# Second attention: bias, scale and row maximum with the sink in one VectorE instruction per head, and pairs of heads begun one or two chunks apart

## The chip, the core and the metric

The kernel runs on one core of one Trainium2 chip. The metric is the device time of one execution in microseconds (us). Five engines run their own instruction streams and meet through semaphores: TensorE (PE in the profile; its weight loads are PEld), VectorE (DVE), ScalarE (ACT), GpSimd (POOL) and SyncE (SP), which issues the loads of the weights.

## The reference

Two transformer blocks of width 2048 run one after the other on 256 positions, all in float32. The first has two attention branches, gates and a gated network. The second begins with a sliding-window attention of 32 query heads and 8 key heads of 64 values, and that is the part that the change touches:

```python
s = jnp.einsum('bnqhgd,bnshd->bnhgqs', q, kb).astype(jnp.float32) * HEAD_DIM ** -0.5 + bias
s = jnp.where(mask[None, :, None, None], s, -jnp.inf)
```

The bias comes from a table by distance. Each head also has a sink logit, which takes part in the softmax (in its maximum and in its sum) and in nothing else. The scale is 1/8. After it come the output product, a norm, a convolution network and its down product.

## The kernel before, in words

**The stream of weights.** All products with weights are one list of 812 chunks. A chunk is two tiles of 128 x 512 of some weight (1024 floats per partition). SyncE loads it to `raw`; ACT casts it to a rounded copy `whi` (L796); DVE subtracts that from the original to get the rest, `wlo` (L1147); PE multiplies with three matmuls of 512 columns per tile and half of the positions (L1755 to L1757), 12 for a chunk. `whi` and `wlo` have three places each, and so the cast of chunk t+2 waits until PE is through with chunk t-1.

**Side steps.** Everything else is cut into named steps, which `side_steps` puts at chunk numbers. Each engine goes through the chunks in order. At chunk t, ACT and DVE first do the cast and the subtraction of chunk t+2, ACT then empties finished product banks where there are any, and then each does its part of the steps at t, in the order in which they were put. PE does the matmuls of chunk t and then its part of the steps at t. No engine steps over an instruction that waits.

**The second attention.** It works on 16 pairs of heads, in four groups c of four pairs e (pair i = 4c + e). A pair goes through ten steps at ten chunks in a row:

- `pscore`: PE makes the scores in two banks, two heads of 128 x 128 in one and of 128 x 256 in the other (eight matmuls).
- `psoft`: DVE adds scale and bias and takes the maximum (L1494 to L1516). This is the step that is changed.
- `pexp`: ACT makes the exponentials with their sums (L1033) and that of the sink (L1036).
- `pprob`, `pscale`: DVE scales a third of them by 1 over the sum (L1520, L1522, L1158), ACT the rest (L764).
- `pptr`: PE turns six tiles of 128 x 128 in two banks (L1817).
- `ppcp`: ACT copies them out (`PH`), and DVE takes the rest (`PL`, L1529).
- `ppv`: PE multiplies with the values (L1986, L1987).
- `py`, `pz`: ACT and DVE add the two halves (`YS`, L1536) and split the sum (`YH`, `YL`, L1539).

Before each group come `qtr` (PE turns the queries, source `NAT`) and, a chunk later, `qcp` (`QP`, ACT and DVE, four instructions each for the two).

**Four side banks.** Side steps share PSUM banks 4 to 7. `side_banks` hands them out in turn, in the order of the steps, so a new order of the steps also changes who follows whom on a bank. PE waits in front of a use until the reader of the bank's last use is through: `psoft` frees a `pscore` (semaphore `s_pbias`), `ppcp` a `pptr` (`s_pptV`), `py` a `ppv` (`s_ys`), `qcp` a `qtr` (`s_q`).

**Biases.** GpSimd loads the bias tiles of a group to `BT`, which has two places. The loads for groups 2 and 3 wait for `psoft` of the last pair of groups 0 and 1.

Of the kernel before, what the change touches and what calls it, by code (L numbers as in the profile page):

```python
# [12 lines left out]
ALU = mybir.AluOpType  # L13
ACT = mybir.ActivationFunctionType
AX = mybir.AxisListType.X

P = 128
D = 2048
S = 256
# [176 lines left out]
def side_steps(chunks):  # L196
# [3 lines left out]
    def put(t, *step):  # L200
        at[t].append(step)
# [26 lines left out]
    for n in range(16):  # L228
        t0 = (64 if n < 8 else 108) + 3 * (n % 8)
# [60 lines left out]
    for j in range(4):  # L290
        put(478 + j, "ktr", j)
        put(479 + j, "kcp", j)
    for c, (t0, t1) in enumerate(((484, 487), (500, 503), (508, 512), (516, 521))):
        for b in range(2):
            put(t0 + 1, "qtr", 2 * c + b)
        for b in range(2):
            put(t0 + 2, "qcp", 2 * c + b)
        stages = ("pscore", "psoft", "pexp", "pprob", "pscale", "pptr", "ppcp", "ppv", "py", "pz")
        for e in range(4):
            for j, name in enumerate(stages):  # L300
                put(t1 + e + j, name, 4 * c + e)
    put(544, "gain", 2)
    for name, i in (("busy", 0), ("rs", 6), ("update", 0), ("Ttr", 16), ("Ttr", 17), ("Tsp", 16), ("Tsp", 17),
                    ("update", 1), ("sq6", 0)):
# [59 lines left out]
def build(nc, A):  # L364
    ctx = ExitStack()
    with ctx:
# [10 lines left out]
        def sems(names):  # L377
            return [ctx.enter_context(nc.semaphore("s_" + n)) for n in names.split()]
# [73 lines left out]
        SK = sb("SK", [P, 32])  # L452
# [47 lines left out]
        s_sig, s_mix, s_xb = sems("sig mix xb")  # L500

        s_dupA, s_ktr, s_khi, s_k, s_qtr, s_qhi, s_q = sems("dupA ktr khi k qtr qhi q")
        s_psc, s_pbias, s_pmax, s_psink, s_pneg, s_pexp, s_psum, s_prcp, s_ppv = sems(
            "psc pbias pmax psink pneg pexp psum prcp ppv")
        s_pprobV, s_pprobA, s_pptr, s_pptA, s_pptV, s_yt, s_ys, s_yhi2, s_Y2 = sems(
            "pprobV pprobA pptr pptA pptV yt ys yhi2 Y2")
        s_mg, s_upd, s_busy, s_rowd, s_rowm, s_R = sems("mg upd busy rowd rowm R")
# [84 lines left out]
        def side_freed(use):  # L592

            name, i, b = use
            if name == "bias":
                return s_biasln, 1
            if name == "ctr":
                return s_C, 2 * i + 2
            if name == "krtr":
                return s_kr, 2  # L600
            if name == "qktr":
                return s_qk, i + 1
            if name == "score":
                return s_msk, i + 1
            if name == "ptr":
                return s_pt, i + 1
            if name == "pv":
                return s_y, i + 1
            if name == "uqtr":
                return s_uq, i + 1  # L610
            if name == "mktr":
                return s_mk, i + 1
            if name == "mtr":
                return s_M, 2 * i + 2
            if name == "Ttr":
                return s_T, 16 + 2 * i + 2
            if name == "htr":
                return s_H, i + 1
            if name == "ktr":
                return s_k, i + 1  # L620
            if name == "qtr":
                return s_q, 2 * i + 2
            if name == "pscore":
                return s_pbias, 2 * i + 1 + b
            if name == "pptr":
                return s_pptV, 2 * i + 1 + b
            if name == "ppv":
                return s_ys, 2 * i + 2
            if name == "busy":
                return s_busy, i + 1  # L630
            return s_R, 1

        def bt_view(c, e, n):
            base = BT[:, c % 2, 2 * e:2 * e + 2, 0:n]
            pat = [list(z) for z in base.ap]
            pat[-1] = [-1, n]
            return bass.AP(base.tensor, base.offset + n - 1, pat)
# [56 lines left out]
        def gpsimd_program(eng):  # L694
            po = Seat(eng)
# [44 lines left out]
            load_bias(0)  # L740
            load_bias(1)
            row_rstd(5)
            po.wait_ge(s_pbias, 8)
            load_bias(2)
            po.wait_ge(s_pbias, 16)
            load_bias(3)
            po.wait_ge(s_qtr, 8)
            eng.dma_start(GB[:, :], bass.AP(A["norm_g_2"].tensor, D, [[0, P], [1, D]])).then_inc(l_g1, 16)
# [11 lines left out]
        def scalar_program(eng):  # L760
            ac = Seat(eng)
# [128 lines left out]
            def side(name, i, t):  # L890
# [138 lines left out]
                elif name == "pexp":  # L1029
                    s, a = pair_scores(i), AS[:, i % 6, :]  # L1030
                    ac.wait_ge(s_pneg, i + 1)
                    for z, (lo, hi) in enumerate(PAIR_PARTS):
                        eng.activation(s[:, lo:hi], s[:, lo:hi], ACT.Exp, bias=a[:, 12 + z:13 + z], scale=1.0,  # L1033
                                       accum_out=a[:, 8 + z:9 + z]).then_inc(s_pexp, 1)
                    ac.wait_ge(s_psink, 2 * i + 2)
                    eng.activation(a[:, 4:8], a[:, 4:8], ACT.Exp, bias=0.0, scale=1.0).then_inc(s_pexp, 1)  # L1036
                elif name == "pscale":
                    s, a = pair_scores(i), AS[:, i % 6, :]
# [52 lines left out]
            c = 2  # L1091
# [17 lines left out]
        def vector_program(eng):  # L1109
# [209 lines left out]
            def side(name, i, t):  # L1319
# [164 lines left out]
                elif name == "psoft":  # L1484
# [5 lines left out]
                        ve.wait_ge(s_pptr, 2 * (i - 4) + 2)  # L1490
                    else:
                        ve.wait_ge(s_mm, upto[IN2])
                    ve.wait_ge(s_psc, 2 * i + 1)
                    eng.scalar_tensor_tensor(out=s[:, 0:S].rearrange("p (h n) -> p h n", h=2),  # L1494
                                             in0=b0[:, 0:S].rearrange("p (h n) -> p h n", h=2), scalar=0.125,
                                             in1=bt_view(c, e, P), op0=ALU.mult, op1=ALU.add).then_inc(s_pbias, 1)
                    ve.wait_ge(s_psc, 2 * i + 2)
                    eng.scalar_tensor_tensor(out=s[:, S:768].rearrange("p (h n) -> p h n", h=2),
                                             in0=b1.rearrange("p (h n) -> p h n", h=2), scalar=0.125,
                                             in1=bt_view(c, e, S), op0=ALU.mult, op1=ALU.add).then_inc(s_pbias, 1)  # L1500
                    if i >= 6:
                        ve.wait_ge(s_pprobA, 2 * (i - 6) + 2)
                        ve.wait_ge(s_pprobV, 2 * (i - 6) + 2)
                    ve.wait_ge(s_pbias, 2 * i + 1)
                    eng.reduce_max(a[:, 0:2], s[:, 0:S].rearrange("p (h n) -> p h n", h=2), AX).then_inc(s_pmax, 1)
                    ve.wait_ge(s_pbias, 2 * i + 2)
                    eng.reduce_max(a[:, 2:4], s[:, S:768].rearrange("p (h n) -> p h n", h=2), AX).then_inc(s_pmax, 1)
                    av = a[:, 0:4].rearrange("p (t h) -> p t h", t=2)
                    dv = a[:, 4:8].rearrange("p (t h) -> p t h", t=2)
                    sk = SK[:, 2 * i:2 * i + 2].unsqueeze(1).to_broadcast([P, 2, 2])  # L1510
                    ve.wait_ge(s_pmax, 2 * i + 2)
                    ve.wait_ge(l_sk, 16)
                    eng.tensor_tensor(av, av, sk, ALU.max).then_inc(s_psink, 1)
                    ve.wait_ge(s_psink, 2 * i + 1)
                    eng.tensor_tensor(dv, sk, av, ALU.subtract).then_inc(s_psink, 1)
                    eng.tensor_scalar(a[:, 12:16], a[:, 0:4], -1.0, None, ALU.mult).then_inc(s_pneg, 1)  # L1516
                elif name == "pprob":
# [547 lines left out]
def constants():  # L2065

    f = np.float32
    c = np.zeros((P, 560), f)
    c[:, 0:128] = np.eye(P, dtype=f)
    tri = np.where(np.arange(P)[None, :] <= np.arange(P)[:, None], 0.0, NEG).astype(f)  # L2070
    c[:, 128:256] = tri
    c[:, 384:512] = tri
    for o, d in ((512, 32), (528, 64)):
        fr = f(500000.0) ** (-np.arange(0, d, 2, dtype=f) / f(d))
        c[:, o:o + d // 2] = fr.astype(f)[None, :]
    b = np.zeros((32, 768), f)
    b[:, 384:768] = NEG
    for i in range(127, 255):
        n = i - 127
        if n < 16:  # L2080
            k = n
        else:
            k = min(16 + int(f(math.log(n / 16) / math.log(8)) * f(16)), 31)
        b[k, i] = 1.0
        b[:, 384 + i] = 0.0
    return c, b

# [33 lines left out]
```

## Time and profile before

| what | value |
|---|---|
| median of three runs | 2343.35 us |
| the three runs | 2343.95, 2334.42, 2343.35 us |
| profiled execution | 2334.78 us, span 2333.0 us |
| instructions | 29072 |
| PE busy | 2315.2 us, 99% |
| DVE busy | 1619.8 us, 69% |
| ACT busy | 1244.4 us, 53% |
| second attention in the profiled execution | about 1375 to 1541 us |

Busy time is time in which an engine has an instruction under way. The start of one PE or DVE instruction may lie before the end of the one in front, so the distance from start to start, called the pitch here, tells what an instruction costs the queue. The span is 1.8 us shorter than the profiled execution's own time.

### The profile page before, as it was taken

The page shows a single profiled execution, that of the slowest core. Times are in us where ns is not written, and L with a number is a line of the kernel's source. Part 1 is how long each engine was busy: PE and PEld are TensorE (multiplying, and loading weights), DVE is VectorE, ACT ScalarE, POOL GpSimd, SP SyncE. Part 2 cuts the span into 40 slices and gives each one's busy share as a digit, 9 for nine tenths or more (in the row PEclk, how much of TensorE's full clock was granted, in tenths as well). Part 3 has the DMA queues.
Part 4 walks back from the last instruction along what each step waited for, and adds up shares of the span by engine and source line. Part 5 has one row for each costly group of instructions (what it writes and reads, how often), then busy time and mean ns, then how long its engine had stood idle before and what let it go on. Part 6 is the DMA issues. An engine that isn't in the chain of part 4 may idle for free.

```text
span 2333.0 us, 29072 instructions
## 1 busy us (share of the span) xinstructions
PE 2315.2 (99%) x11296; PEld 1953.5 (84%) x11296; DVE 1619.8 (69%) x2291; ACT 1244.4 (53%) x1847; POOL 21.2 (1%) x34
## 2 busy tenths in 40 slices
PE   9999999999999999999999999999999999999998
PEld 7888888888888888888888888888888888888887
DVE  6445565665787787786565677977888888885444
ACT  7445454555655555555454567866444444444343
POOL 1000000000000000000000000000000000000000
PEclk9999999999999999999999999999999999999999
DMA  8665555656655656656656666455666666666665
GB/s 270 192 188 172 156 172 153 187 184 189 217 180 186 220 171 202 214 165 194 208 188 194 210 187 185 147 160 176 193 189 192 190 190 189 192 189 192 195 192 162
DMA packets 226425, 439.29 MB, mean 188 GB/s; under 512 B 13632, under 2 KB 17888, under 8 KB 225904
## 3 DMA queue, kind: packets, MB, share of 16 engines
q1 hardware_dynamic: 224400, 429.51, 59.6%
q0 software_dynamic: 1888, 7.93, 1.1%
q8 instruction: 89, 1.46, 0.3%
q14 instruction: 48, 0.39, 0.1%
HBM read 435.24 MB, written 2.15 MB: 187 GB/s over the span
## 4 chain that ended last, share of the span: by engine, by line
PE 95%; DVE 3%; ACT 1%; issue 1%; DMA 0%; SPq 0%; DVEq 0%; POOLq 0%; POOL 0%; ACTq 0%
PE bank L1757 22%; PE bank L1755 22%; PE bank L1756 22%; PE bank L1805 14%; PE bank L1807 7%; PE bank L1817 2%; PE bank L1725 2%; PE bank L1728 2%; PE bank L1726 2%; DVE wlo L1147 1%; ACT whi L796 1%; DMA raw<-in_w_in_dram 0%; PE bank L1860 0%; ACT S2b L1033 0%; PE bank L1877 0%
## 5 line engine op out<-in xcount | busy, mean ns | idle before, releaser
L1147 DVE TENSOR_TENSOR wlo<-raw,whi 128x1024 fp32r<-128x1024 f32 (+2 forms) x660 | 801.8, 1216 | 566.1 <-ACT whi L796 565.0
L796 ACT CAST whi<-raw 128x1024 fp32r<-128x1024 f32 (+2 forms) x660 | 688.2, 1043 | 871.0 <-PE bank L1757 618.4
L1805 PE MATMUL bank<-TT,whi 128*128 128x512 f32 x1408 | 488.9, 391 | 0.8 <-DVE TT L1409 0.8
L1755 PE MATMUL bank<-whi,TT 128*128 128x512 f32 (+1 forms) x1172 | 461.3, 394 | 1.7 <-DVE wlo L1147 1.0
L1757 PE MATMUL bank<-whi,TT 128*128 128x512 f32 (+1 forms) x1172 | 454.5, 388 | 0.0
L1756 PE MATMUL bank<-wlo,TT 128*128 128x512 f32 (+1 forms) x1172 | 453.9, 387 | 0.0
L1807 PE MATMUL bank<-TT,wlo 128*128 128x256 f32 x1408 | 394.1, 280 | 0.0
L1805 PEld LDWEIGHTS bank<-TT,whi 128*128 128x128 f32 x1408 | 263.3, 187 | 58.9 <-issue 1.3
L1807 PEld LDWEIGHTS bank<-TT,wlo 128*128 128x128 f32 x1408 | 266.1, 189 | 0.0
L1755 PEld LDWEIGHTS bank<-whi,TT 128*128 128x128 f32 x1172 | 220.2, 188 | 46.2 <-DVE wlo L1147 1.9
L1757 PEld LDWEIGHTS bank<-whi,TT 128*128 128x128 f32 x1172 | 219.9, 188 | 45.4
L1756 PEld LDWEIGHTS bank<-wlo,TT 128*128 128x128 f32 x1172 | 220.3, 188 | 42.8
L1147 DVE TENSOR_TENSOR wlo<-RX,whi 128x1024 fp32r<-128x1024 f32 x97 | 118.6, 1223 | 71.0 <-ACT whi L796 70.7
L796 ACT CAST whi<-RX 128x1024 fp32r<-128x1024 f32 x97 | 102.0, 1052 | 103.4 <-DMA RX<-in_w_up_dram 49.5
L1755 PE MATMUL bank<-whi,FH 128*128 128x512 f32 x352 | 137.4, 390 | 0.0
L1757 PE MATMUL bank<-whi,FH 128*128 128x512 f32 x352 | 137.0, 389 | 0.0
L1756 PE MATMUL bank<-wlo,FH 128*128 128x512 f32 x352 | 137.0, 389 | 0.0
L1757 PE MATMUL bank<-whi,Hl 128*128 128x512 f32 x340 | 132.3, 389 | 0.0
L1756 PE MATMUL bank<-wlo,Hh 128*128 128x512 f32 x340 | 132.3, 389 | 0.0
L1755 PE MATMUL bank<-whi,Hh 128*128 128x512 f32 x340 | 132.3, 389 | 0.0
L1756 PEld LDWEIGHTS bank<-wlo,FH 128*128 128x128 f32 x352 | 66.1, 188 | 13.6
L1755 PEld LDWEIGHTS bank<-whi,FH 128*128 128x128 f32 x352 | 66.1, 188 | 13.6
(298 smaller groups left out, 3028.7 us busy)
## 6 DMA issues: line engine op xcount, KB each, us to landing
raw<-in_ffn_w_up_dram SPq DMA_DIRECT2D x176, 512.0 KB, 3.6
raw<-in_w_in_dram SPq DMA_DIRECT2D x120, 512.0 KB, 3.7
raw<-in_w_down_dram SPq DMA_DIRECT2D x88, 512.0 KB, 4.7
raw<-in_ffn_w_down_dram SPq DMA_DIRECT2D x88, 512.0 KB, 4.7
RX<-in_w_gate_dram SPq DMA_DIRECT2D x66, 512.0 KB, 4.0
RX<-in_w_up_dram SPq DMA_DIRECT2D x66, 512.0 KB, 4.2
raw<-in_swa_w_in_dram SPq DMA_DIRECT2D x48, 512.0 KB, 3.7
raw<-in_w_out_dram SPq DMA_DIRECT2D x32, 512.0 KB, 4.0
```

The lines of the kernel that those rows point to most:

```text
L796: eng.copy(parted(hi_at(u), src), src).then_inc(s_cast, 1)
L1147: eng.tensor_tensor(parted(lo_at(u), src), src, parted(hi_at(u), src).bitcast(F32), ALU.subtract).then_inc(s_lo, 1)
L1725: eng.matmul(o[:, :], lh, hi[:, b, :], start=fresh, stop=False)
L1726: eng.matmul(o[:, :], lh, lo[:, b, :], start=False, stop=False)
L1728: mm = eng.matmul(o[:, :], ll, hi[:, b, :], start=False, stop=read)
L1755: eng.matmul(o, lh[:, ts], hi[:, kk, :], start=start, stop=False)
L1756: eng.matmul(o, lh[:, ts], lo[:, kk, :], start=False, stop=False)
L1757: mm = eng.matmul(o, ll[:, ts], hi[:, kk, :], start=False, stop=stop)
L1805: eng.matmul(o[:, :], hi[:, kk, fs], TT[:, k, :, :].rearrange("p a s -> p (a s)"), start=k == 0, stop=False)
L1807: mm = eng.matmul(o[:, 0:S], lo[:, kk, fs], Th[:, k, :], start=False, stop=k == KT - 1)
L1817: return eng.transpose(out, src, ident[:, :])
```

## The change

`psoft` did seven DVE instructions for a pair: scale and bias for two banks, two maxima, the maximum with the sink, and two small ones. Now it does one `tensor_tensor_reduce` for each of four parts (head and bank), which adds score and bias, scales by 1/8, and takes the maximum with the sink as its start value, and then the two small ones. The bias table is stored eight times as large, so that one scale serves both. The semaphore `s_pmax` goes, and the counts that others wait for are changed to match.

The four pairs of a group began at chunks 487 to 490, 503 to 506, 512 to 515 and 521 to 524. They now begin at 487, 489, 491, 493; 503, 504, 506, 508; 511, 512, 514, 516; and 519, 520, 522, 524. The queries of the third and fourth group are turned at 509 and 517, as before.

```diff
-    for c, (t0, t1) in enumerate(((484, 487), (500, 503), (508, 512), (516, 521))):
+    for c, (t0, begin) in enumerate(((484, (487, 489, 491, 493)), (500, (503, 504, 506, 508)),
+                                     (508, (511, 512, 514, 516)), (516, (519, 520, 522, 524)))):
...
-                put(t1 + e + j, name, 4 * c + e)
+                put(begin[e] + j, name, 4 * c + e)
...
-                return s_pbias, 2 * i + 1 + b
+                return s_pbias, 4 * i + 2 + 2 * b
...
-            po.wait_ge(s_pbias, 8)
-            load_bias(2)
             po.wait_ge(s_pbias, 16)
+            load_bias(2)
+            po.wait_ge(s_pbias, 32)
             load_bias(3)
...
-                    ac.wait_ge(s_psink, 2 * i + 2)
+                    ac.wait_ge(s_psink, i + 1)
...
-                    ve.wait_ge(s_psc, 2 * i + 1)
-                    eng.scalar_tensor_tensor(out=s[:, 0:S].rearrange("p (h n) -> p h n", h=2),
-                                             in0=b0[:, 0:S].rearrange("p (h n) -> p h n", h=2), scalar=0.125,
-                                             in1=bt_view(c, e, P), op0=ALU.mult, op1=ALU.add).then_inc(s_pbias, 1)
-                    ve.wait_ge(s_psc, 2 * i + 2)
-                    eng.scalar_tensor_tensor(out=s[:, S:768].rearrange("p (h n) -> p h n", h=2),
-                                             in0=b1.rearrange("p (h n) -> p h n", h=2), scalar=0.125,
-                                             in1=bt_view(c, e, S), op0=ALU.mult, op1=ALU.add).then_inc(s_pbias, 1)
...
-                    ve.wait_ge(s_pbias, 2 * i + 1)
-                    eng.reduce_max(a[:, 0:2], s[:, 0:S].rearrange("p (h n) -> p h n", h=2), AX).then_inc(s_pmax, 1)
-                    ve.wait_ge(s_pbias, 2 * i + 2)
-                    eng.reduce_max(a[:, 2:4], s[:, S:768].rearrange("p (h n) -> p h n", h=2), AX).then_inc(s_pmax, 1)
+                    ve.wait_ge(l_sk, 16)
+
+                    for z, (lo, hi) in enumerate(PAIR_PARTS):
+                        t, h = divmod(z, 2)
+                        n = hi - lo
+                        ve.wait_ge(s_psc, 2 * i + 1 + t)
+                        eng.tensor_tensor_reduce(out=s[:, lo:hi], in0=(b0, b1)[t][:, h * n:h * n + n],
+                                                 in1=bt_view(c, e, n)[:, h, :], scale=0.125,
+                                                 scalar=SK[:, 2 * i + h:2 * i + h + 1], op0=ALU.add, op1=ALU.max,
+                                                 accum_out=a[:, z:z + 1]).then_inc(s_pbias, 1)
...
-                    ve.wait_ge(s_pmax, 2 * i + 2)
-                    ve.wait_ge(l_sk, 16)
-                    eng.tensor_tensor(av, av, sk, ALU.max).then_inc(s_psink, 1)
-                    ve.wait_ge(s_psink, 2 * i + 1)
+                    ve.wait_ge(s_pbias, 4 * i + 4)
                     eng.tensor_tensor(dv, sk, av, ALU.subtract).then_inc(s_psink, 1)
...
-        b[k, i] = 1.0
+        b[k, i] = 8.0
```

**DVE, `psoft` of pair 8.** `S2a` is where the scores are kept, `AS` holds the small per-row values, `BT` the bias, `SK` the sinks. Before, seven instructions:

```order
L1494 SCALAR_TENSOR_TENSOR S2a_86<-bank4,BT_85 128x256 [waits s_psc,s_pptr,s_bt0]
L1498 SCALAR_TENSOR_TENSOR S2a_86<-bank5,BT_85 128x512 [waits s_psc]
L1505 TENSOR_REDUCE AS<-S2a_86 128x2 [waits s_pbias,s_pprobV,s_pprobA]
L1507 TENSOR_REDUCE AS<-S2a_86 128x2 [waits s_pbias]
L1513 TENSOR_TENSOR AS<-AS,SK 128x4 [waits s_pmax]
L1515 TENSOR_TENSOR AS<-SK,AS 128x4 [waits s_psink]
L1516 TENSOR_SCALAR AS<-AS 128x4
```

The same place of the changed kernel:

```order
L1503 ISA S2a_86,AS<-bank5,BT_85,SK 128x128 [waits s_pprobV,s_pprobA,s_psc,s_pptr,s_bt0]
L1503 ISA AS 128x1
L1503 ISA S2a_86,AS<-bank5,BT_85,SK 128x128
L1503 ISA AS 128x1
L1503 ISA S2a_86,AS<-bank6,BT_85,SK 128x256 [waits s_psc]
L1503 ISA AS 128x1
L1503 ISA S2a_86,AS<-bank6,BT_85,SK 128x256
L1503 ISA AS 128x1
L1511 TENSOR_TENSOR AS<-SK,AS 128x4 [waits s_pbias]
L1512 TENSOR_SCALAR AS<-AS 128x4
```

Each of the four new instructions comes as two: the pass over the part, and one that writes the row's maximum. A pair has ten DVE instructions in place of seven.

**PE, in front of the scores of pair 8.** `PH` and `PL` are the turned probabilities, `VV` the values, `KH`, `KL`, `QP` keys and queries. Before, this stands at chunk 512 (`ppv` of pair 6, then `pscore` of pair 8):

```order
L1986 MATMUL bank7<-PH_88,VV_81 128x512 [waits s_pptV]
L1987 MATMUL bank7<-PH_88,VV_81 128x2x128
L1986 MATMUL bank7<-PL0_89,VV_81 128x512
L1987 MATMUL bank7<-PL0_89,VV_81 128x2x128
L1961 MATMUL bank4<-KH_78,QP_82 128x128 [waits s_ys]
L1962 MATMUL bank4<-KL_79,QP_82 128x128
L1961 MATMUL bank4<-KH_78,QP_82 128x128
L1962 MATMUL bank4<-KL_79,QP_82 128x128
L1961 MATMUL bank5<-KH_78,QP_82 128x256 [waits s_pptV]
```

Of the changed kernel, at chunk 511 (the end of `ppv` of pair 5, `pptr` of pair 6, `pscore` of pair 8):

```order
L1983 MATMUL bank6<-PL1_90,VV_81 128x2x128
L1813 MATMUL bank7<-ident,S2b_87 128x128 [waits s_pprobA,s_pprobV,s_q]
L1813 MATMUL bank7<-ident,S2b_87 128x128 x3
L1813 MATMUL bank4<-ident,S2b_87 128x128 [waits s_q]
L1813 MATMUL bank4<-ident,S2b_87 128x128
L1957 MATMUL bank5<-KH_78,QP_82 128x128 [waits s_ys]
L1958 MATMUL bank5<-KL_79,QP_82 128x128
L1957 MATMUL bank5<-KH_78,QP_82 128x128
L1958 MATMUL bank5<-KL_79,QP_82 128x128
L1957 MATMUL bank6<-KH_78,QP_82 128x256 [waits s_ys]
```

The second half of the scores now goes to bank 6, which `ppv` of pair 5 has filled in the same stop of PE, and waits on `s_ys` until `py` of pair 5 has read it.

**DVE, at the beginning of chunk 512 of the changed kernel.** `py` of pair 5 is the two rows that read bank 6:

```order
L1148 TENSOR_TENSOR wlo<-raw,whi 128x1024 [waits s_cast]
L1535 TENSOR_TENSOR YL_84<-YS_91,YH_83 128x256 [waits s_yhi2]
L1532 TENSOR_TENSOR YS_91<-bank6,YS_91 64x256 [waits s_yt]
L1532 TENSOR_TENSOR YS_91<-bank6,YS_91 64x256
L1525 TENSOR_TENSOR PL0_89<-bank7,PH_88 128x512 [waits s_pptA]
```

They stand behind the subtraction of chunk 514, whose cast waits for PE to be through with chunk 511. The same arrangement is at chunk 519, where the scores of pair 12 wait for `py` of pair 9 of chunk 520.

## Rows read from the trace of the kernel before

**Rows 1.** The page's first part: busy time, share and instructions of each engine.
```profile
PE 2315.2 (99%) x11296; PEld 1953.5 (84%) x11296; DVE 1619.8 (69%) x2291; ACT 1244.4 (53%) x1847; POOL 21.2 (1%) x34
```

**Rows 2.** Waits of PE over the run: total us, times, longest.
```profile
PE bank L1817 <- DVE PL L1529: 4.9, 5, 1.4
```

**Rows 3.** Busy time by stretch, second attention: us, busy (count) per engine, PEclk, DMA, GB/s.
```profile
1375.00:1541.00 166.00, 161.09 (x841) 136.30 (x841) 143.51 (x311) 131.89 (x321) 2.37 (x3) 1.00 0.52 161
```

**Rows 4.** Timeline of PE, three of the five waits: start, us, [idle before <-releaser].
```profile
1455.97 1.09 PE L1817 MATMUL bank<-ident,NAT 128*128 128x128 f32 x8 [1.13 <-DVE PL L1529]
...
1492.49 0.87 PE L1817 MATMUL bank<-ident,S2a 128*128 128x128 f32 x6 [1.35 <-DVE PL L1529]
...
1498.49 0.44 PE L1817 MATMUL bank<-ident,S2b 128*128 128x128 f32 x2 [1.23 <-DVE PL L1529]
```

**Rows 5.** The chain that ended last, one piece: start, us, what.
```profile
1486.57 0.61 DVE AS L1507
```

**Rows 6.** Timeline of DVE, `psoft` of pair 0.
```profile
1381.03 0.43 DVE L1494 SCALAR_TENSOR_TENSOR S2a<-bank,BT 128x256 f32<-128x256 f32 x1
1381.38 0.68 DVE L1498 SCALAR_TENSOR_TENSOR S2a<-bank,BT 128x512 f32<-128x512 f32 x1
1381.97 0.41 DVE L1505 TENSOR_REDUCE AS<-S2a 128x2 f32<-128x256 f32 x1
...
1383.21 0.16 DVE L1515 TENSOR_TENSOR AS<-SK,AS 128x4 f32<-128x4 f32 x1
...
1383.44 1.23 DVE L1147 TENSOR_TENSOR wlo<-raw,whi 128x1024 fp32r<-128x1024 f32 x1
```

**Rows 7.** Timeline of ACT, one `pexp` and the cast behind it.
```profile
1446.26 0.40 ACT L1033 ACTIVATE S2b<-S2b,AS 128x128 f32<-128x128 f32 x1
1446.57 0.19 ACT L1033 ACTIVATION_READ_ACCUMULATOR S2b<-S2b,AS 128x1 f32 x1
1446.66 0.39 ACT L1033 ACTIVATE S2b<-S2b,AS 128x128 f32<-128x128 f32 x1
...
1448.13 1.06 ACT L796 CAST whi<-raw 128x1024 fp32r<-128x1024 f32 x1
```

**Rows 8.** Timeline of DVE: `pprob`, a subtraction, `ppcp`, `py`.
```profile
1456.16 0.15 DVE L1520 TENSOR_TENSOR AS<-AS 128x4 f32<-128x4 f32 x1
...
1456.96 1.22 DVE L1147 TENSOR_TENSOR wlo<-raw,whi 128x1024 fp32r<-128x1024 f32 x1
1458.10 1.02 DVE L1529 TENSOR_TENSOR PL<-bank,PH 128x512 fp32r<-128x512 f32 x2
...
1463.28 0.88 DVE L1536 TENSOR_TENSOR YS<-bank,YS 64x256 f32<-64x256 f32 x2
```

**Rows 9.** Timeline of ACT: `ppcp`, `pscale`, `qcp`, `py`, `pz`, a bank emptied.
```profile
1453.96 0.86 ACT L764 ACTIVATE PH<-bank 128x512 fp32r<-128x512 f32 x2
1454.71 0.90 ACT L764 ACTIVATE S2b<-S2b,AS 128x256 f32<-128x256 f32 x2
...
1458.00 2.45 ACT L764 ACTIVATE QP<-bank 64x512 fp32r<-64x512 f32 x4
...
1461.42 0.78 ACT L764 ACTIVATE YS<-bank 64x256 f32<-64x256 f32 x2
...
1464.98 0.41 ACT L764 ACTIVATE YH<-YS 128x256 fp32r<-128x256 f32 x1
...
1498.06 1.09 ACT L764 ACTIVATE PR<-bank 128x512 f32<-128x512 f32 x2
```

**Rows 10.** Timeline of PE: a chunk from first matmul to side step; `ppv`, then `pptr`.
```profile
1451.18 0.48 PE L1755 MATMUL bank<-whi,TT 128*128 128x512 f32 x1
...
1454.02 0.82 PE L1817 MATMUL bank<-ident,S2a 128*128 128x128 f32 x6
...
1459.65 0.39 PE L1986 MATMUL bank<-PH,VV 128*128 128x512 f32 x1
...
1460.34 0.82 PE L1817 MATMUL bank<-ident,S2b 128*128 128x128 f32 x6
```

More of the change, by code:

```diff
@@ L502, in build @@
         s_dupA, s_ktr, s_khi, s_k, s_qtr, s_qhi, s_q = sems("dupA ktr khi k qtr qhi q")
-        s_psc, s_pbias, s_pmax, s_psink, s_pneg, s_pexp, s_psum, s_prcp, s_ppv = sems(
-            "psc pbias pmax psink pneg pexp psum prcp ppv")
+        s_psc, s_pbias, s_psink, s_pneg, s_pexp, s_psum, s_prcp, s_ppv = sems(
+            "psc pbias psink pneg pexp psum prcp ppv")
         s_pprobV, s_pprobA, s_pptr, s_pptA, s_pptV, s_yt, s_ys, s_yhi2, s_Y2 = sems(
@@ L742, in gpsimd_program @@
             row_rstd(5)
-            po.wait_ge(s_pbias, 8)
+            po.wait_ge(s_pbias, 16)
             load_bias(2)
-            po.wait_ge(s_pbias, 16)
+            po.wait_ge(s_pbias, 32)
             load_bias(3)
```

## The prediction

> **What bounds the kernel now.** I read the page's busy times first: PE is busy for 2315.2 us of a span of 2333.0, DVE for 1619.8 and ACT for 1244.4 [rows 1]. So work taken from DVE is worth only what PE now waits for it. I looked for those waits next. In the whole run PE waits for the second attention five times, 4.9 us in all, each time a group of transposes (L1817) for the second instruction set of `ppcp` (L1529) to free a bank [rows 2]. The stretch of the second attention says the same: 166.0 us long, PE busy 161.1, so 4.9 idle, while DVE is busy for 143.5 and ACT for 131.9, at a granted clock of 1.00 [rows 3]. Both helpers have little to spare there, and only there does it matter that they run in order. Three of the five waits stand in the timeline: 1.13 us in front of the queries' transposes (chunk 509), 1.35 in front of those of pair 9 (chunk 518), 1.23 in the middle of those of pair 11 (chunk 520) [rows 4]. The other two are of pairs 3 and 15. They arise where `pptr` of a pair takes the bank that `ppcp` of the pair before leaves in the same chunk. Ahead of the wait at 1492 the chain runs through the row maxima of `psoft` [rows 5], so a shorter `psoft` does reach the bound in places.
>
> From this comes a cap that holds for the whole change: PE's instructions are the same in number and kind, only their order differs. All that can be won is the 4.9 us, 0.21% of the run. A measurement of this kernel tells a difference from none at about 0.5%, 11.7 us: its three runs differ by 9.5 us. The profiled execution took 2334.8 us, near the lowest of them and 8.6 below the median, so I work out a difference against it and add that to the median.
>
> **`psoft` on DVE.** Seven instructions take 2.41 us from start to start (1381.03 to 1383.44). The two passes that add the bias have pitches of 0.35 us for 256 columns and 0.59 for 512, so about 0.94 ns a column and 0.11 us for each instruction [rows 6]. The new instruction reads the same operands (bank and bias), so I price it by that: 0.23 us for 128 columns, 0.35 for 256, 1.16 for two of each. No DVE row shows the reading of a row's result. The nearest is ACT's: 0.19 us long, but 0.09 from its start to that of the next (1446.57 to 1446.66) [rows 7]. Four of them are 0.36. The two small instructions at the end keep their 0.23 [rows 6], and they wait for the last maximum, some 0.1. Sum 1.85 us, 0.56 less than now. Bounds: with reads that cost nothing it is 1.5 us, 0.9 less; with no overlap at all, each pass at the full 0.43 of a 256-column row (0.30 for 128) and each read at 0.19, 2.55, 0.14 more. I take 0.5 less, since DVE rows of this kernel do overlap: 8 us of DVE's 143.5 over 16 pairs. Since it is DVE's time, it is worth nothing by itself.
>
> A rule speaks against many small instructions. The Trainium skill, "VectorE: DVE Perf Modes", the section on the TRN2 errata, says that Vector instructions pay a fixed cost each (120 cycles with a PSUM source, 58 with an SBUF source, at 0.96 GHz) and advises tiles of 512 or more. By its formula the old seven are an estimated 2.16 us and the new ten 1.68, 0.5 less: the fixed cost is paid more often, but 768 columns are gone over once and not twice. So here the rule and my sum from rows give the same.
>
> **Loads and other waits.** The bias loads for groups 2 and 3 start behind `psoft` of pairs 3 and 7, now chunks 494 and 509 for 491 and 507; they are wanted at 512 and 520, over 10 chunks of at least 2.8 us [rows 10] later. I price that at nothing; if the cover were gone, DVE would wait for what is left of a transfer. SyncE's loads are not moved against anything. GpSimd has only the waits in front of those loads. ACT does the same instructions.
>
> **The moved steps: who follows whom on a bank.** I went through the four side banks in both orders. In the old order the waits of the kind "reader's step in the same chunk as the new use" come mostly from pairs that follow at one chunk. In the new order pairs two chunks apart lose them: the waits of pairs 3, 11 and 15 (1.23 for pair 11) should go. Pairs 5, 9 and 13 still follow at one chunk and have theirs, at chunks 509, 517 and 525, and at 509 and 517 the queries' transposes now wait for `psoft` of pair 7 and 11 (the last thing that DVE does in that chunk) where they waited for `ppcp`. DVE has to do there: subtraction 1.14 behind a cast of 0.95, `ppcp` 1.0, `pprob` 0.8 [rows 8], half of the new `psoft` 0.6, 4.5 us together. PE arrives after the last chunk's side steps (1.6), 2.8 of matmuls and 0.66 of `pptr` [rows 10], 5.1. So these waits are nothing while ACT is on time, and up to some 2 us each where it is a step late: at 516, ACT has a cast, two emptied banks 1.1, `py` 0.8, `pscale` 0.8 [rows 9] and `pexp` 1.87 [rows 7], 5.5 us in all, and PE 4.3. I take 1.0, 1.4 and 0.3 for the three places, with bounds of 1.0 and 4.7 for their sum.
>
> What is new is a use ahead of its reader. At chunk 511 the second half of the scores of pair 8 goes to the bank that `ppv` of pair 5 filled just before, and its reader `py` is a step of chunk 512; at 519 it is so for pair 12 and `py` of pair 9. Queued behind that wait are PE's other scores and the whole of the next chunk. When PE is through with the matmuls of 511, ACT must still cast chunk 514 (0.95 to 1.06), split pair 4 (0.41) and copy for pair 5 (0.78) [rows 9]; DVE must subtract (1.14), split (0.35) and add twice (0.9) [rows 8]: cast 1.05, subtraction to 2.2, split to 2.6, addition to 3.5. PE has 0.69 of `ppv`, some 0.66 of `pptr` (six at a pitch of 0.11, from the row of 0.82 for six with the last one's tail) and, at the same pitch, 0.45 of scores to do meanwhile, 1.8 [rows 10]. So it waits at least 1.7 us. At 519 ACT also empties two product banks (1.05) [rows 9], which brings `py` to 4.2 and the wait to 2.4. Together 4.1 us at least. At most: at 510 and 518 ACT has cast, `ppcp` 0.75, `pscale` 0.8, `pexp` 1.87 and `qcp` 2.45 [rows 7, 9], 6.8 us against 3.4 of PE, of which about half is made good in the next chunk, so up to 1.5 to 2 more at each: 7.
>
> **Sum.** New waits 4.1 to 7, take 5.7; left of the old kind 1.0 to 4.7, take 2.7; together 8.4 against 4.9 now: 3.5 us longer. Bounds of the case: 5.1 - 4.9 = 0.2 and 11.7 - 4.9 = 6.8 us longer. Profiled 2334.8 + 3.5 = 2338.3; on the median 2343.35 + 3.5 = 2346.9 us, rounded 2347.
>
> **Rivals.**
>
> *The waits vanish* (chance 0.22). If the two waits at 511 and 519 are covered, as when PE comes there late because it waited elsewhere, and the smoother order leaves ACT and DVE ahead, PE's idle time in the stretch falls to near 1 us: 3.9 less, 2339.5 us. For it: `psoft` stands on the chain [rows 5] and shrinks, and with pairs two chunks apart ACT never has two `pexp` in following chunks with a `qcp` behind. Against it: the casts of 514 and 522 cannot begin before PE stands at the wait, whatever the rest does.
>
> *The new instruction is slow* (0.13). If it takes two cycles a column where the passes take one, `psoft` gains 768 x 0.94 ns = 0.72 us on my price and lasts 2.57 or, with no overlap, 3.3. Over the 13 pairs in the tight part that is up to 13 x 1.2 = 15 us over my forecast, of which DVE has 22.5 of idle time to hide some [rows 3]: it decides once `psoft` is longer than the 2.41 of today. I put it at 10 us slower than before, 2353. Against it: the subtraction of the chunks reads two SBUF tensors of float32 at 1.22 us for 1024 columns [rows 8], full rate, and the new one has one source in PSUM.
> The Trainium skill, "Vector Engine (DVE) Microarchitecture Reference", points that are easy to get wrong, says that an instruction with accumulator readback and two SBUF sources that are not bf16 halves its throughput; by its letter it does not bear on a PSUM source.
>
> *Nothing moves* (0.15). The new and the lost waits come out even, within 1 us of before: 2343.
>
> **The numbers.** Forecast 0.50, the others as given. Faster by over 0.5% is beyond the cap of 4.9 us in every case and comes only from runs that fall unevenly: 0.04. Slower by over 0.5% needs more than 11.7 us: half of the slow instruction and a cascade in the forecast's tail, 0.09. The same: 0.87. The range takes 2343.35 less the cap and less the spread to the lowest run in part, 2333, and plus 12, 2356.
>
> **What the profile of after would show.** (1) DVE rows of L1503 with pitches of about 0.23 and 0.35 us and reads of about 0.09; `psoft` 1.7 to 2.0 us; DVE busy for some 8 us less, but more instructions by 48. (2) PE waits at two scores groups (L1957) for `YS` (L1532), 1.7 to 3.7 us each, at chunks 511 and 519. (3) Waits of L1813 for L1525 fewer than five, and one or two on L1503. (4) PE idle in the stretch 5 to 12 us. The prediction is wrong if (2) is missing, if PE idles less than 4 us or over 13 in the stretch, or if another stretch changes.

## The result, and the profile after

The changed kernel takes 2346.53 us (median of 20 runs, 2345.62 to 2356.80), the kernel before 2334.83 (median of 20 runs, 2333.96 to 2343.95). The ratio is 1.0043 with a 95% interval of 1.0031 to 1.0054, so the change costs 7 to 13 us. The profiled executions say the same: 2346.43 against 2334.78, 11.65 us longer. The ratio is still within the 0.5% that the prediction calls "the same", but the interval excludes 1.

Runs of both kernels come in two clusters some 9.3 us apart (here near 2334.5 and 2343.6). Two of the three runs shown ahead of the prediction lay in the upper one. This matters for the verdict on the forecast: 2347 was met by luck, because its base, 2343.35, was of the upper cluster. On the median of 20 runs, 2334.83, the same forecast gives 2338.3. The forecast difference was 3.5 us, the measured one 11.7. One run of one experiment below took 3906 us, at a mean granted clock of 0.56, for a reason that stays open; the interval given there leaves it out.

The first part of the page after; it answers to [rows 1].

```profile
PE 2320.8 (99%) x11296; PEld 1956.8 (83%) x11296; DVE 1610.6 (69%) x2339; ACT 1244.9 (53%) x1847; POOL 21.1 (1%) x34
```

DVE has 48 instructions more and is busy for 9.2 us less, much as forecast. But PE is busy for 5.6 us **more**, with the same 11296 instructions. No term of the forecast allows for that. The waits of PE after (total, times, longest), which answer to [rows 2]:

```profile
PE bank L1957 <- DVE YS L1532: 4.5, 2, 2.5
PE bank L1813 <- DVE PL L1525: 3.6, 3, 1.4
PE bank L1813 <- DVE AS L1503: 3.1, 5, 1.2
```

11.2 us where there were 4.9. Now the second attention by itself, from the start of its first score matmul to that of the second network's first matmul. First of before, then of after (the stretch's bounds, its length, then busy time of PE, PEld, DVE, ACT, POOL with counts, PEclk, DMA share, GB/s):

```profile
1378.44:1594.12 215.68, 210.02 (x1078) 177.07 (x1076) 172.42 (x349) 156.54 (x361) 3.08 (x4) 1.00 0.53 164
```
```profile
1378.14:1605.88 227.74, 215.62 (x1077) 180.57 (x1076) 162.84 (x397) 157.00 (x361) 3.08 (x4) 0.98 0.50 155
...
1470.00:1476.00 6.00, 5.84 (x24) 4.93 (x25) 2.71 (x13) 1.08 (x3) 0.00 (x0) 0.72 0.24 84
...
1509.00:1513.00 4.00, 3.50 (x11) 3.03 (x12) 3.04 (x13) 1.17 (x4) 0.00 (x0) 0.57 0.40 131
```

The stretch holds the whole difference: it is 12.1 us longer, and it starts and is followed as before. Its length splits into two parts that can be read off each row: idle time (length less PE busy) went from 5.7 to 12.1 us, +6.4, and PE's busy time from 210.0 to 215.6, +5.6, for the same matmuls. DVE's busy time fell by 9.6 us, which PE does not get. The PEclk column (the granted clock of PE, 1.00 is full speed) says where the busy time grew: 1.00 over the stretch before, 0.98 after, and in short pieces 0.72 and 0.57. One such piece in the timeline of PE (start, us, what, [idle before <-releaser]):

```profile
1470.16 0.39 PE L1957 MATMUL bank<-KH,QP 128*128 128x256 f32 x1 [1.96 <-DVE YS L1532]
...
1471.21 0.39 PE L1753 MATMUL bank<-whi,TT 128*128 128x512 f32 x1
1471.44 0.55 PE L1751 MATMUL bank<-whi,TT 128*128 128x512 f32 x1
1471.78 0.63 PE L1752 MATMUL bank<-wlo,TT 128*128 128x512 f32 x1
...
1474.77 0.47 PE L1753 MATMUL bank<-whi,TT 128*128 128x512 f32 x1
1475.08 0.22 PE L1957 MATMUL bank<-KH,QP 128*128 128x128 f32 x1
```

This is chunk 511. The second half of pair 8's scores waits 1.96 us for `YS` (`py` of pair 5), the wait that the forecast placed there. Some 1.3 us after it the pitch of the 512-column matmuls goes from 0.23 to 0.43 us for 3.6 us and then comes back; such a stretch is called a fall of the clock below. A pitch of 0.43 for 0.23 is the granted clock at its lower level, 1.2 for 2.4 GHz. The nine matmuls from 1471.44 take 3.64 us instead of 2.05, a loss of 1.6. The other two places, behind the waits of chunks 509 and 519:

```profile
1458.12 1.11 PE L1813 MATMUL bank<-ident,NAT 128*128 128x128 f32 x4 [0.15 <-DVE AS L1503]
1458.88 0.78 PE L1751 MATMUL bank<-whi,TT 128*128 128x512 f32 x1
1459.46 0.63 PE L1752 MATMUL bank<-wlo,TT 128*128 128x512 f32 x1
...
1509.50 0.58 PE L1957 MATMUL bank<-KH,QP 128*128 128x256 f32 x1 [2.51 <-DVE YS L1532]
...
1510.52 0.63 PE L1751 MATMUL bank<-whi,YH 128*128 128x512 f32 x1
```

Counted in the same way they lose 1.5 and 1.4 us in 3.3 and 3.1 us; at 519 the fall begins with the first matmul behind the wait. Three falls are 4.5 of the 5.6 us. Of the rest, 1.1, most can be put down to the counting: a matmul in front of a wait is busy for its whole 0.39 us, where its pitch is 0.23, and there are ten waits for banks for five before, an estimated 0.8 us. In the run before, the PEclk of this stretch is 1.00, and there is no fall. The Trainium skill, "TensorE: Matmul & The Clock Gate", the section on single-matmul spacing ("Wait — 56ns, not 53.3ns?"), gives 426.7 ns between 512-column matmuls at the lower level and 215.7 at the upper; the trace agrees on the first (0.43 us) and shows 0.23 for the second.

The new instruction, `psoft` of pair 0 on DVE; it answers to [rows 6]:

```profile
1380.73 0.35 DVE L1503 CUSTOM_DVE_ANT_0 S2a<-bank,BT,SK 128x128 f32<-128x128 f32 x1
1381.01 0.08 DVE L1503 DVE_READ_ACCUMULATOR2_ANT AS<- 128x1 f32 x1
1381.01 0.35 DVE L1503 CUSTOM_DVE_ANT_0 S2a<-bank,BT,SK 128x128 f32<-128x128 f32 x1
...
1381.28 0.48 DVE L1503 CUSTOM_DVE_ANT_0 S2a<-bank,BT,SK 128x256 f32<-128x256 f32 x1
1381.68 0.08 DVE L1503 DVE_READ_ACCUMULATOR2_ANT AS<- 128x1 f32 x1
```

Each reading of a result starts at the same 0.01 us as the next pass, so it adds no step of its own. The passes have pitches of 0.27 and 0.40 us (forecast 0.23 and 0.35); whether the readings have a part in these extra 0.04 and 0.05 us is not shown. A whole `psoft`, from its first pass to DVE's next instruction, takes 1.62 us (1456.63 to 1458.25).

### The profile page after: what moved, and what is told of

Same layout as the page of the kernel before. It is cut to its first block, busy times and chain, and to the rows that moved or that the text cites. A ratio compares the mean times of both kernels' runs of the same rounds, so it can differ in the third digit from the quotient of the medians.

```text
span 2344.6 us, 29119 instructions
## 1 busy us (share of the span) xinstructions
PE 2320.8 (99%) x11296; PEld 1956.8 (83%) x11296; DVE 1610.6 (69%) x2339; ACT 1244.9 (53%) x1847; POOL 21.1 (1%) x34
## 4 chain that ended last, share of the span: by engine, by line
PE 96%; ACT 2%; DVE 1%; DMA 0%; issue 0%; SPq 0%; DVEq 0%; POOLq 0%; POOL 0%; ACTq 0%
PE bank L1751 22%; PE bank L1753 22%; PE bank L1752 22%; PE bank L1801 14%; PE bank L1803 7%; PE bank L1813 2%; PE bank L1721 2%; PE bank L1724 2%; PE bank L1722 1%; DVE wlo L1148 0%; ACT whi L797 0%; DMA raw<-in_w_in_dram 0%; PE bank L1856 0%; ACT S2b L1034 0%; PE bank L1873 0%
```

## The experiments

All stand beside the kernel before, which had medians of 2334.89 and 2334.46 in the two sets. For each the same row is shown: from the first score matmul of the second attention to the first matmul of the second network. Idle is its length less PE's busy time. Theory A is that the bank waits made by the new starts cost their own length and a fall of the clock behind it.

**The new instruction with the old starts.**

```diff
-    for c, (t0, begin) in enumerate(((484, (487, 489, 491, 493)), (500, (503, 504, 506, 508)),
-                                     (508, (511, 512, 514, 516)), (516, (519, 520, 522, 524)))):
+    for c, (t0, begin) in enumerate(((484, (487, 488, 489, 490)), (500, (503, 504, 505, 506)),
+                                     (508, (512, 513, 514, 515)), (516, (521, 522, 523, 524)))):
```

> The fused instruction alone, the pairs at their old chunks. Theory A (the new starts make the loss, the fused instruction is a gain): psoft lasts 1.6 us for 2.4 before; of the 4.9 us that PE waited in the second attention 2 to 3 are left, no fall of the clock; the profiled time is 2 to 3 us under before, about 2332. Theory B (the fused instruction makes the loss, by where it puts DVE's work): at least 5 us of the 11.6 us lost stay, 2340 or more.

Measured: 2332.38 us, ratio 0.9975 [0.9961, 0.9989]: 2.5 us faster than before and 14 faster than the changed kernel.

```profile
PE bank L1813 <- DVE PL L1525: 3.1, 3, 1.2
```
```profile
1378.08:1591.82 213.74, 209.80 (x1078) 177.21 (x1076) 162.66 (x397) 156.07 (x361) 3.08 (x4) 1.00 0.53 165
```

PE busy 209.8, idle 3.9. The time and the waits are those of Theory A; Theory B is out. The instruction is a gain by itself, and of the 5.7 us that PE idled before 3.9 are still there: the shorter `psoft` reaches the bound at some waits only.

**The old instructions with the new starts.** The seven instructions of `psoft` from the kernel before, with the changed table of starts.

> The old seven instructions of psoft, the pairs at the new chunks. Theory A: every wait of the changed kernel is there and those behind psoft are up to 0.8 us longer: PE waits 12 to 14 us in the second attention and there are three or more falls of the clock, 2347 to 2351 us. Theory B: most of the loss is gone, 2340 us or less.

Measured: 2350.34 us, ratio 1.0052 [1.0032, 1.0072].

```profile
PE bank L1962 <- DVE YS L1537: 6.8, 4, 2.6
...
PE bank L1818 <- DVE S2b L1495: 3.0, 3, 1.8
```
```profile
1378.50:1610.40 231.90, 217.88 (x1078) 181.24 (x1076) 172.81 (x349) 157.46 (x361) 3.08 (x4) 0.97 0.49 152
...
1513.00:1518.00 5.00, 5.00 (x15) 4.03 (x15) 2.96 (x9) 0.00 (x0) 0.00 (x0) 0.50 0.29 99
```

Idle 14.0, busy 7.9 over before. Time and waits (13.2 us) are within the expectation, but there are two falls of the clock where three or more were expected, and each is longer than any of the changed kernel: 6.1 and 6.0 us, 2.8 and 2.7 us lost by pitch. They stand behind waits of 2.63 and 2.64 us in front of the second half of the scores of pairs 8 and 12, each with another wait of 0.73 and 0.77 us just ahead of it. Behind a wait of 1.81 us at chunk 494 there is none.

With the one above this makes a square: the instruction gains 2.5 us with the old starts and 3.8 with the new ones; the starts cost 15.5 with the old instructions and 14.2 with the new one. The whole loss is the starts'.

**One bank ahead of its reader less.** The second half of pair 8's scores goes to a product bank that is idle then, and PE waits for that one instead.

```diff
+                if use == ("pscore", 8, 1):
+                    bank[use] = 0
...
-                if side_before[use]:
+                if use == ("pscore", 8, 1):
+                    pe.wait_ge(*emptied_at(("in2", 4), 0))
+                elif side_before[use]:
```

> The changed kernel with one use moved: the second half of the scores of pair 8 goes to product bank 0, idle from chunk 508 to 515, so that PE needs not wait at chunk 511 for py of pair 5. Theory A: the wait of 1.96 us is gone and with it the fall of the clock right behind it (about 1.7 us), 3 to 4 us under the changed kernel, about 2343. If the wait only goes elsewhere: the bank's next user waits instead, and the time is that of the changed kernel within 1 us. If the fall does not belong to the wait: 2 us less only.

Measured: 2343.02 us, ratio 1.0024 [1.0009, 1.0040], 3.5 us less than the changed kernel.

```profile
PE bank L1819 <- DVE PL L1529: 3.6, 3, 1.4
PE bank L1819 <- DVE AS L1507: 3.0, 4, 1.2
PE bank L1963 <- DVE YS L1536: 2.4, 1, 2.4
```

```profile
1378.31:1602.80 224.49, 214.39 (x1078) 179.38 (x1076) 162.90 (x397) 157.19 (x361) 3.08 (x4) 0.98 0.51 157
```
```profile
1458.71 0.47 PE L1755 MATMUL bank<-whi,TT 128*128 128x512 f32 x1
...
1493.55 1.12 PE L1819 MATMUL bank<-ident,NAT 128*128 128x128 f32 x4 [0.15 <-DVE AS L1507]
...
1494.90 0.63 PE L1756 MATMUL bank<-wlo,YH 128*128 128x512 f32 x1
```

The wait at 511 is gone, and the others, 509 and 519 among them, keep their sizes. Taking away a wait of 1.96 us gained 3.5 us; in the stretch, idle time is 2.0 us less and PE's busy time 1.2. But the falls did not stay where they were. The changed kernel has them behind the waits of 509, 511 and 519, this one behind those of 517 and 519. At 509 PE's idle times are the same in both (0.95 or 0.94, 0.80 and 0.15 us), and here there is no fall behind them; at 517 they are the same too (1.41 or 1.40, 0.80, 0.15), and here there is one, of 1.5 us. So one wait less made one fall less, but Theory A had the place wrong for the others: the length of waits alone does not say whether the clock falls.

**The waits filled with work.** Products of the identity with itself ahead of the waits. They are added work; nothing is left out.

```diff
...
+                if use in fills:
+                    st, g, n = fills[use]
+                    pe.wait_ge(*emptied_at((st, g), 0))
+                    o = bank[banks[st, g][0]]
+                    for _ in range(n):
+                        eng.matmul(o[:, 0:P], ident[:, :], ident[:, :], start=True, stop=True)
```

> The changed kernel with 76 small matmuls of 0.11 us (identity times identity, into a product bank that nobody uses at that time) in front of eight of PE's waits, each group some tenths shorter than the wait, so that the order and the waits stay but PE has something to do. Theory A1 (some 5 us of the loss are the granted clock that falls behind PE's idle time, and the waits cost only their own 11.2): the clock stays at 1.00, idle time falls under 5 us and the time is about 5 us under the changed kernel, 2341. Theory A2 (the falls have nothing to do with PE's idle time): granted clock 0.97 in the stretch as now, 2346 or, with the fillers, more.

Measured: 2345.78 us, ratio 1.0049 [1.0031, 1.0066]. Each such product in float32 leaves two records at a pitch of 0.11 us, so the 76 take 17 us and not half of it as planned. They overfill the waits, and the time comes out near that of the changed kernel: by itself it does not price the waits. What it does show is the clock, 1.00 over the whole stretch:

```profile
1377.70:1604.60 226.90, 225.94 (x1230) 194.40 (x1229) 163.02 (x397) 157.00 (x361) 3.08 (x4) 1.00 0.50 156
```

So it was repeated with 44 products, fewer at each wait.

> The changed kernel with 44 extra products of the identity with itself, each 0.22 us of PE by the first filled run, put where its waits stand and sized to them (5 at chunk 494, 12 at 509 and 510, 8 at 511, 9 at 517, 10 at 519, 5 at 525; 9.8 us for 11.2 of waits). They write into an idle product bank that the next group overwrites; nothing is left out. Theory A (11.2 us of waits plus some 5.3 us in which the granted clock stands at 0.50 behind them): no fall left in the attention, the waits' time stays as work, so 5 us under the changed kernel, 2341 to 2342.5. Rival B (the granted clock falls on its own account, or costs nothing because PE would wait anyway): the time stays within 1.5 us of 2346.5.

Measured: 2342.89 us, ratio 1.0037 [1.0026, 1.0049], 3.6 us under the changed kernel, where 4 to 5.5 were expected.

```profile
1378.10:1601.99 223.89, 221.16 (x1165) 187.51 (x1164) 162.82 (x397) 157.03 (x361) 3.08 (x4) 1.00 0.51 158
```
```profile
1457.29 0.65 PE L1823 MATMUL bank<-ident,NAT 128*128 128x128 f32 x4
1458.10 0.66 PE L1823 MATMUL bank<-ident,NAT 128*128 128x128 f32 x4 [0.15 <-DVE AS L1503]
...
1458.82 0.39 PE L1752 MATMUL bank<-wlo,TT 128*128 128x512 f32 x1
```

PE does 9.7 us of useless work and the kernel is faster for it. At chunk 509 the transposes and the chunk behind them stand at the very times of the changed kernel (1457.29 there 1457.31, 1458.10 there 1458.12), yet the next 512-column matmuls are at the short pitch. Rival B fell with this: the helpers are as late as before, and only PE's idling was taken away. Against the changed kernel the stretch is 3.9 us shorter: idle time 9.4 us less, 9.7 us of fillers, and 4.1 us less of PE's other busy time, near the 4.5 of the three falls. PE's busy time less the fillers is 211.5 us, still 1.5 over before; that part was not traced.

**The new starts for groups 1 and 2 alone.**

```diff
-                                     (508, (511, 512, 514, 516)), (516, (519, 520, 522, 524)))):
+                                     (508, (512, 513, 514, 515)), (516, (521, 522, 523, 524)))):
```

> The changed kernel with the new starts for the first two groups of pairs alone; groups 3 and 4 begin as before the change, a pair a chunk. The new instruction stays. Theory A (the cost is made by banks that are taken ahead of their reader): the first groups bring the wait of 1.2 us at chunk 494, and at 509 and 510 the same three waits as the changed kernel (1.9 us), and one bank ahead of its reader is left, at 513 (second half of pair 9's scores on the bank of ppv of pair 6, read at 514), so one wait of some 2 us with a fall of the clock of some 1.5 behind it; 519 has none. Waits 7 to 9 us, time 2339 to 2343. Rival C (it is the late groups alone that cost): 2332 to 2335, as with the old starts.

Measured: 2338.68 us, ratio 1.0011 [1.0002, 1.0021].

```profile
PE bank L1813 <- DVE PL L1525: 3.5, 3, 1.3
PE bank L1813 <- DVE AS L1503: 2.0, 2, 1.2
PE bank L1957 <- DVE YS L1532: 1.5, 1, 1.5
```
```profile
1378.23:1598.09 219.86, 211.98 (x1077) 178.25 (x1076) 163.12 (x397) 156.64 (x361) 3.08 (x4) 0.99 0.52 161
...
1458.00:1464.00 6.00, 6.00 (x25) 4.91 (x24) 5.22 (x11) 5.26 (x15) 0.88 (x1) 0.74 0.65 198
```

6.3 us over the version with the old starts, so rival C (only the late groups cost) falls. The early groups bring the wait at 494, the later `psoft` of pair 7 in front of the queries at 509 with its fall (0.74), and the wait at 513. That one is 1.5 us, less than the 2 expected, and has no fall behind it; with that fall missing, the time is 0.3 us under the lower end of Theory A.

**The two waits added.** The version with the old starts, and PE made to wait, ahead of the second half of the scores of pairs 8 and 12, for `py` of a step of the next chunk.

```diff
                         b0 = take("pscore", i, t)
+                        if t and i in (8, 12):
+                            pe.wait_ge(*side_freed(("ppv", i - 2, 0)))
```

> The new instruction with the old starts (2332.4 us) and two waits added on PE, of the kind that the new starts bring: ahead of the second half of the scores of pairs 8 and 12 (chunks 512 and 521) PE waits for py of pairs 6 and 10, a step of the next chunk. Nothing else differs. Theory A (such a wait costs its own length and a fall of the granted clock behind it): two waits of 1.7 to 2.7 us, the clock at 0.50 for some 3 us behind each, together 6 to 8.5 us on top: 2338.5 to 2341. Rival B (a wait costs its length and no more, the clock falls for another reason): 3.5 to 5 us on top, 2336 to 2337.5, granted clock near 1.00.

Measured: 2340.90 us, ratio 1.0025 [1.0013, 1.0036], 8.5 us over the version with the old starts.

```profile
PE bank L1959 <- DVE YS L1532: 5.2, 2, 2.6
PE bank L1813 <- DVE PL L1525: 3.1, 3, 1.2
```
```profile
1378.08:1600.14 222.06, 212.97 (x1078) 179.52 (x1076) 162.88 (x397) 156.05 (x361) 3.08 (x4) 0.98 0.52 159
```
```profile
1470.87 0.55 PE L1959 MATMUL bank<-KH,QP 128*128 128x256 f32 x1 [2.58 <-DVE YS L1532]
...
1471.86 0.63 PE L1751 MATMUL bank<-whi,TT 128*128 128x512 f32 x1
```

This is the cleanest of all: the same kernel with two waits. Idle time +5.2, PE's busy time +3.2; the stretch is 8.3 us longer, of 8.5 us in the run's time. The two falls lose 1.4 and 1.3 us by pitch. Two falls of the clock, one behind each wait, and they begin with the first matmul behind it. So waits alone bring such falls; nothing else of the changed kernel is needed.

**The queries of groups 3 and 4 split.** The version with the old starts, with the second query's transposes and their copy a chunk later than the first's.

```diff
-            put(t0 + 1, "qtr", 2 * c + b)
+            put(t0 + (1 + b * (c > 1)), "qtr", 2 * c + b)
...
-            put(t0 + 2, "qcp", 2 * c + b)
+            put(t0 + (2 + b * (c > 1)), "qcp", 2 * c + b)
```

> A try at a version better than both: the new instruction and the old starts, and for groups 3 and 4 the second query's transposes (qtr) and their copy (qcp) one chunk later than the first's, so that ACT has one copy of 1.2 us in a chunk and not two, and the bank uses shift by one. No bank is taken ahead of its reader. Theory A (three waits of 3.1 us in all are left in the version with the old starts, two of them at 509 and 517 where PE has arrived at the banks of the pair before): one or two of them shrink, the time is 2330 to 2332.5. Rival D (the waits only move to the next group that uses a bank in the same chunk): 2332 to 2333.5, the sum of waits 3 us or more.

Measured: 2331.79 us, ratio 0.9993 [0.9980, 1.0006].

```profile
PE bank L1813 <- DVE PL L1525: 1.8, 2, 1.1
```
```profile
1377.97:1590.84 212.87, 210.05 (x1078) 177.05 (x1076) 162.91 (x397) 155.82 (x361) 3.08 (x4) 1.00 0.54 166
```

One of the three waits is gone, and the stretch is 0.9 us shorter than with the old placing, the best of all. Its median is the lowest too, but this interval touches 1, so on times it isn't told from the kernel before; the version without the split is the one that is.

## Why the forecast was right and wrong

| step of the prediction | forecast | measured |
|---|---|---|
| `psoft` | 1.85 us, bounds 1.5 to 2.55 | 1.62 |
| DVE busy | some 8 us less, +48 instructions | 9.2 less, +48 |
| old kind of waits left (509, 517, 525) | 1.0, 1.4, 0.3 | 1.90, 2.36, 1.23 |
| new waits at 511 and 519 | 5.7 together, bounds 4.1 to 7 | 1.96 and 2.51 |
| sum of the waits | 8.4, bounds 5.1 to 11.7 | 11.2 |
| matmuls themselves | unchanged | 5.6 us longer |
| difference | +3.5, bounds +0.2 to +6.8 | +11.7 |

Of the signs that the prediction named, the new waits (2), PE's idle time (4) and DVE's busy time came within or near what was said; `psoft` at 1.62 us is just under its 1.7, and there are five waits of L1813 on L1503 for the "one or two" of sign (3).

**Right: the cap and the place.** The instruction alone gave 2.5 us of a cap of 4.9, and no other stretch moved. The use ahead of its reader at 511 and 519, and whom it waits for, came as forecast; the rival in which these waits vanish is out, and so are the slow instruction and "nothing moves".

**`psoft`: a total within its bounds, from two errors.** The passes are dearer than priced (1.35 us against 1.16 for the four), and the readings, priced at 0.36 from ACT's row [rows 7], add nothing to that. Neither was to be read from the rows of before. The Trainium skill, "VectorE: DVE Perf Modes", the section on the TRN2 errata, has a formula (120 cycles with a PSUM source and one a column, at 0.96 GHz) that would have been nearer: an estimated 0.26 and 0.39 us, where the trace has 0.27 and 0.40. The prediction had worked out 1.68 us for the whole step by it, and kept its own 1.85. The price of the slow-instruction rival has a slip of its own: from a forecast near 1.9 us to its 3.3 is 1.4 us a pair, not 1.2. The rival did not come true, so nothing hangs on it.

**Mis-sized: the old kind of wait.** The forecast took 2.7 us for three places; they are 5.5, above the bound of 4.7. The row behind 509 shows the cause:

```profile
1455.64 0.87 PE L1813 MATMUL bank<-ident,S2a 128*128 128x128 f32 x6 [0.95 <-DVE PL L1525]
1457.31 0.65 PE L1813 MATMUL bank<-ident,NAT 128*128 128x128 f32 x4 [0.80 <-DVE AS L1503]
```

The forecast knew that the queries' transposes would now follow `psoft`, but counted one wait for a chunk. There are three in a row: `pptr` for `ppcp`, then each query's transposes for one half of `psoft`, which DVE begins only when `ppcp` and `pprob` are done. PE's arrival does not count for the later ones, since PE has only a group of transposes between them. A further wait was overlooked, at 494, where the second half of `pptr` of pair 1 takes the bank that `psoft` of pair 3 reads in that chunk:

```profile
1404.56 0.44 PE L1813 MATMUL bank<-ident,S2a 128*128 128x128 f32 x2 [1.21 <-DVE AS L1503]
```

**Failed: that a wait costs its length.** The sentence "PE's instructions are the same in number and kind, only their order differs. All that can be won is the 4.9 us" holds for a gain. The forecast used it for the loss as well, and summed only waits. Behind three of the places PE ran for some 3 us at half clock, a loss of 4.5 of the 5.6 us of busy time added; the filled waits and the added waits show it from both sides. The Trainium skill, "TensorE: Matmul & The Clock Gate", the section on psum-queue depth-cycling, tells of a kernel whose PE idles between groups as it goes round its banks, and whose clock swings between its two levels. The trace agrees (PEclk 0.72 and 0.57 behind the waits for banks); the forecast should have made it a rival.

**By bounds.** 11.2 us of waits lay within the bounds of the waits; +11.7 lay outside the bounds of the difference (+0.2 to +6.8), by the missing term. That the time itself came out at 2347 is luck: the base was 8.5 us too high, and the difference 8.2 us too small.

**Left open.** What a wait must be like for the clock to fall behind it. The seven single waits of 1.96 to 2.64 us in these runs each had a fall behind them; the single waits of up to 1.81 us had none. But of three waits in a row the same ones had a fall in one kernel and none in another: 1.9 us in all at 509 (a fall in the changed kernel, none with one wait less) and 2.35 us in all at 517 (none in the changed kernel, one with one wait less). So lengths alone do not decide. In the attention's stretch of all ten profiled executions the falls stand only behind waits; what else they need no run isolates.

## What to carry to other kernels

When the order of steps changes on the engine that is the bound, write down for each use of a shared bank in which step its last reader stands: a use ahead of that step is a wait. Time the two halves of such a change apart: here the faster instruction gained 2.5 us and the new order lost 14. Do not price a wait on TensorE at its length alone: here each fall of the clock behind one cost 1.3 to 1.6 us more, and 2.7 and 2.8 where a wait of 0.7 us stood just ahead of one of 2.6. A rise of PE's busy time with an equal count of instructions is the sign of it.

## What the runs showed of the hardware

- **The clock.** Behind single waits of 1.96 to 2.58 us the granted clock stood at 0.50 for 3.0 to 3.7 us, 1.3 to 1.6 us lost each time when counted by pitch; with the old instructions and the new starts, behind waits of 2.63 and 2.64 us, for 6.1 and 6.0 us, 2.8 and 2.7 us lost. Useless products in the waits kept it at 1.00. Equal waits at 509 and at 517 had a fall in one kernel and none in another.
- **The result register of DVE.** Reading it lasts 0.08 us and starts with the next pass; it adds no step of its own. ACT's adds 0.09 us [rows 7].
- **The two clusters of times.** The 9.3 us between them have nothing to do with the change. In the profile of the version with the split queries, which is of the upper cluster, the second network's first part takes 500.4 us (1590.8 to 2091.2), in the kernel before 491.3 (1594.1 to 2085.4), at a granted clock of 1.00 in both. The median duration of its matmuls is 398 ns against 391 (min/median/max below, before first). Why stays open.

```profile
L1805 PE MATMUL bank<-TT,whi x1408: 391/391/476, 1594.1 to 2085.4; 128*128 128x512 f32 x176
```
```profile
L1801 PE MATMUL bank<-TT,whi x1408: 391/398/478, 1590.8 to 2091.2; 128*128 128x512 f32 x176
```
